# Gate and up products of a feed-forward layer: eight block products replaced by seven with sums

## The reference

```python
def swiglu_ffn(h, wg, wu, wd):
    return (jax.nn.silu(h @ wg) * (h @ wu)) @ wd

# in layer i, for prompt rows (p) and sample rows (s)
fp = swiglu_ffn(xp * (1 + sc2p) + sh2p, ffn_w_gate[i], ffn_w_up[i], ffn_w_down[i])
xp = layer_norm(ALPHA * xp + g2p * fp, ln_ffn_g[i], ln_ffn_b[i])
```

## Time and profile before

| | us |
|---|---|
| three runs | 3110.47, 3113.08, 3115.78 |
| median | 3113.08 |
| span of the profiled execution | 3114.0 |
| busy in the span: PE | 3020.4 |
| DVE | 1431.8 |
| POOL | 1509.5 |
| ACT | 557.7 |

### The profile page before, as it was taken

How to read it: one execution, slowest core, us unless ns; L and a number is a source line. 1 busy time by engine, 2 the same in 40 slices (tenths; PEclk the granted TensorE clock), 3 DMA queues, 4 the chain that set the end, 5 groups by cost and what they waited for, 6 DMA issues and landing times.

```text
span 3114.0 us, 53016 instructions
## 1 busy us (share of the span) xinstructions
PE 3020.4 (97%) x22084; PEld 2794.3 (90%) x22084; DVE 1431.8 (46%) x2529; ACT 557.7 (18%) x1125; POOL 1509.5 (48%) x889
## 2 busy tenths in 40 slices
PE   6999999999999999999989999999999999999997
PEld 4799999999976899999986689999997999999997
DVE  3254652434554752424665545332463536634243
ACT  2220140000220430000234323000022211400001
POOL 2455446545566455545420145554544464455554
PEclk8999999999999999999999999999999999999999
DMA  6642353323345443333321434343322323222221
GB/s 238 223 116 85 119 174 99 107 91 114 90 122 156 152 164 125 132 124 127 87 64 52 116 121 149 128 135 129 116 68 85 100 84 93 80 82 84 82 82 65
DMA packets 450477, 354.81 MB, mean 114 GB/s; under 512 B 26121, under 2 KB 424833, under 8 KB 437934
## 3 DMA queue, kind: packets, MB, share of 16 engines
q1 hardware_dynamic: 435744, 324.79, 32.6%
q10 hardware_dynamic: 14493, 26.63, 2.8%
HBM read 337.86 MB, written 5.25 MB: 110 GB/s over the span
## 4 chain that ended last, share of the span: by engine, by line
issue 33%; PE 30%; POOL 24%; POOLq 10%; DVE 2%; ACT 1%; DVEq 0%; ACTq 0%
PE pb L980 29%; POOL w_lo L890 22%; POOLq L889 10%; POOL prod L916 1%; POOL diag L899 1%; PE pb L1745 0%; PE pb L1702 0%; DVE a_lo L2277 0%; POOLq L945 0%; POOL w_hi L887 0%; POOL yt L946 0%; POOL a_lo L936 0%; DVE xa L2436 0%; DVE pb L2429 0%; PE pb L1624 0%
## 5 line engine op out<-in xcount | busy, mean ns | idle before, releaser
L887 POOL TENSOR_SCALAR w_hi<-w_raw 128x1024 fp32r<-128x1024 f32 (+2 forms) x416 | 449.4, 1080 | 1326.7 <-DMA w_raw<-in_ffn_w_up 399.9
L890 POOL TENSOR_TENSOR w_lo<-w_raw,w_hi 128x1024 fp32r<-128x1024 f32 (+2 forms) x416 | 989.1, 2378 | 69.0 <-issue 69.0
L980 PE MATMUL pb<-h_hi,w_hi 128*128 128x288 f32 x3584 | 946.1, 296 | 10.6 <-DVE xa L2399 3.8
L980 PE MATMUL pb<-h_lo,w_hi 128*128 128x288 f32 x3584 | 927.1, 295 | 0.0
L980 PEld LDWEIGHTS pb<-h_hi,w_hi 128*128 128x128 f32 x3584 | 661.8, 188 | 21.7 <-issue 8.6
L980 PEld LDWEIGHTS pb<-h_lo,w_hi 128*128 128x128 f32 x3584 | 657.6, 188 | 0.0
L980 PE MATMUL pb<-a_hi,w_hi 128*128 128x288 f32 x2176 | 592.9, 297 | 8.1 <-DVE a_lo L2277 5.6
L980 PE MATMUL pb<-a_lo,w_hi 128*128 128x288 f32 x2176 | 587.0, 294 | 0.0
L980 PE MATMUL pb<-h_hi,w_lo 128*128 128x288 f32 x3584 | 560.3, 295 | 0.5
L980 PEld LDWEIGHTS pb<-h_hi,w_lo 128*128 128x128 f32 x3584 | 504.3, 188 | 2.0 <-POOL w_lo L890 1.5
L980 PEld LDWEIGHTS pb<-a_hi,w_hi 128*128 128x128 f32 x2176 | 408.0, 188 | 17.0 <-DVE a_lo L2277 6.7
(11 more groups left out here) (324 smaller groups left out, 2678.9 us busy)
## 6 DMA issues: line engine op xcount, KB each, us to landing
ada_w<-in_ada_w SPq DMA_DIRECT2D x80, 1024.0 KB, 8.0
w_raw<-in_ffn_w_gate SPq DMA_DIRECT2D x88, 512.0 KB, 3.8
w_raw<-in_ffn_w_up SPq DMA_DIRECT2D x88, 512.0 KB, 3.7
w_raw<-in_gmlp_w_in SPq DMA_DIRECT2D x64, 512.0 KB, 4.0
w_raw<-in_ffn_w_down SPq DMA_DIRECT2D x64, 512.0 KB, 3.5
w_raw<-in_gmlp_w_out SPq DMA_DIRECT2D x32, 512.0 KB, 4.5
w_raw<-in_ffn_w_down SPq DMA_DIRECT2D x32, 384.0 KB, 3.1
w_raw<-in_conv_w_pw SPq DMA_DIRECT2D x24, 512.0 KB, 4.0
```

Of the source, the lines that this page charges most:

```text
L887: nc.gpsimd.tensor_scalar(w_hi[:, s, 0:w], w_raw[:, s, 0:w], 1.0, 1.0, ALU.mult, ALU.mult).then_inc(split_hi, 1)
L890: nc.gpsimd.tensor_tensor(w_lo[:, s, 0:w], w_raw[:, s, 0:w], w_hi[:, s, 0:w].bitcast(F32), ALU.subtract).then_inc(split_lo, 1)
L980: return nc.tensor.matmul(out, lhsT, rhs, start=start, stop=stop)
```

## The change

Tiles 0 to 2 of a layer stay as they are, except that tile 2 does its second token half first. From tile 3 on (19 tiles in a layer), the gate and up products of a tile are one product of 2x2 blocks. The weights of a tile are four blocks: the channel halves (four channel tiles each) of gate (g1, g2) and of up (u1, u2). The tokens are four blocks as well: channel half times token half. Eight block products of 4 × 3 matmuls become seven, 84 matmuls in place of 96, by sums of blocks ahead of the products and sums of products behind them:

- weight sums: s1 = u1 + u2, s2 = s1 − g1, s3 = g1 − u1, s4 = g2 − s2
- token sums, once for a layer: t1, t2, t3, t4 in the same pattern; t2 takes the place of the first four channel tiles of the second token half
- products, in the order of PE: p1 = g1·x (first channel and token half), p6 = s2·t2, p5 = s1·t1, p7 = s3·t3, p2 = g2·x (second channel half), p3 = s4·x, p4 = u2·t4
- outputs: c11 = p1 + p2; u23 = p1 + p6; u4 = u23 + p5; c12 = u4 + p3; u23 += p7; c22 = u23 + p5; the fourth is p4 + u23. c11 and c12 are gate, the others up.

DVE makes the weight sums (`form_sums`, `form_last`; s1 and s2 in PSUM banks) and the lower parts of s1 and s2 (`form_low`); ACT makes all upper parts and, in `gated_upper`, those of the gated tile; POOL makes the other five lower parts of 512 words. For the paired tiles POOL no longer makes `w_hi` and `w_lo` of 1024 words. Their units go round slots 0 to 3, the fifth slot holds the sums' parts. Of the token sums DVE makes t1, t3 and t2 and two lower parts, between the splits of tiles 0 and 1 and the gating of tile 2; POOL makes t4 in two operations of 1152 and the lower parts of t3 and t4. DVE also does the sums of products, the gating and the gated tile's lower part (`gated_lower`), in the next tile's turn.

The ada ring becomes four buffers, with other places for its products: four at an FFN's start, then bursts of two to four behind three to five of the tiles, 12 bursts in all. Down products take the last tile of their group late (`late=1`). The residual's scaling on ACT is spread over the first group. The diff, cut to its core; `forms_early` and `forms_late` run on POOL, `form_product` on PE, the loop with `s4_hi` (in `ffn_gates`) on ACT, the rest behind it on DVE, the last lines at each FFN's start:

```diff
-ADA0, ADA1 = 3, 5
+ADA0, ADA1 = 3, 4
...
-ADA_FIRST = 5
+ADA_FIRST = 4
+PAIRED_FROM = 3
+QK = KT // 2
+HALF_UNIT = UNIT // 2
...
+                s = (self.last + 1) % SLOTS
+                if paired and s == SLOTS - 1:
+                    s = 0
...
+            def sums_end(self):
+                self.held[SLOTS - 1] = ("after", (acc_ready, self.products))
...
+            def forms_early(l, m, q):
+                sg_, su = [plan.slot[u] for u in paired_units(l, m)]
+                pool.wait_ge(form_sum, 4 * q + 3)
+                pool.wait_ge(form_hi, 6 * q + 1)
+                lower(w_lo[:, sg_, 0:HALF_UNIT], w_raw[:, sg_, 0:HALF_UNIT], w_hi[:, sg_, 0:HALF_UNIT], form_lo_pool)
+                pool.wait_ge(form_hi, 6 * q + 5)
+                for e in range(2):
+                    part_ = slice(e * HALF_UNIT, (e + 1) * HALF_UNIT)
+                    lower(w_lo[:, su, part_], w_raw[:, su, part_], w_hi[:, su, part_], form_lo_pool)
+            def forms_late(l, m, q):
+                sg_, _ = [plan.slot[u] for u in paired_units(l, m)]
+                pool.wait_ge(form_sum, 4 * q + 4)
+                lower(w_lo[:, sg_, HALF_UNIT:], w_raw[:, sg_, HALF_UNIT:], w_hi[:, sg_, HALF_UNIT:], form_lo_pool)
+                pool.wait_ge(form_hi, 6 * q + 6)
+                lower(s4_lo[:], s4_raw[:], s4_hi[:], form_lo_pool)
...
+                    for m in ms:
+                        forms_late(l, m, FQ.n)
...
+                        FQ.up()
+                        if m != ms[-1]:
+                            forms_early(l, m + 1, FQ.n)
...
+            def form_product(i, wh, wl, xh, xl, lo_made):
+                b = acc_bank()
+                for k in range(QK):
+                    for e, x in enumerate((xh, xl)):
+                        mm(pb[:, b, 0:HALF], wh(k), x(k), k == 0 and e == 0, False)
+                pe.wait_ge(*lo_made)
+                for k in range(QK):
+                    last = mm(pb[:, b, 0:HALF], wl(k), xh(k), False, k == QK - 1)
...
-                        down(count)
+                        down(count, late=1)
                 if l + 1 < DEPTH:
-                    down_norm(GU[2][1])
+                    down_norm(GU[2][1], late=1)
...
+                for m in ms:
+                    act.wait_ge(form_sum, 4 * FQ.n + 4)
+                    fn(s4_hi[:], s4_raw[:], ACT.Copy).then_inc(form_hi, 1)
...
+                    act.wait_ge(acc_ready, G.n + 1)
+                    fn(sg[:, 0, :], pb[:, G.n % BANKS, 0:HALF], ACT.Copy).then_inc(pair_kept, 1)
+                    if m != ms[0]:
+                        gated_upper(m - 1 - first)
...
+                    if m != ms[-1]:
+                        upper_gate(l, m + 1)
+                        upper_up(l, m + 1)
+                        upper_sums(l, m + 1, FQ.n + 1)
+                    for e in range(2):
+                        act.wait_ge(acc_free, BANKS + G.n + 5 + e)
+                        fn(sg[:, e, :], sg[:, e, :], ACT.Silu).then_inc(sg_ready, 1)
...
+                v.tensor_tensor(pb[:, b_1, :], u1, w_raw[:, s_u, HALF_UNIT:], ALU.add).then_inc(form_sum, 1)
+                dve.wait_ge(raw_full[s_g], landed[ug])
+                dve.drain()
+                v.tensor_tensor(pb[:, b_2, :], pb[:, b_1, :], g1, ALU.subtract).then_inc(form_sum, 1)
+                v.tensor_tensor(u1, g1, u1, ALU.subtract).then_inc(form_sum, 1)
...
+            def gated_lower(m):
+                for h in (1, 0):
+                    dve.wait_ge(gated_hi, AH.up())
+                    v.tensor_tensor(one(a_lo, m, half_cols(h)), pr[:, h, :], one(a_hi, m, half_cols(h)).bitcast(F32),
+                                    ALU.subtract).then_inc(a_ready, 1)
...
+            def paired(l, m, ms, first):
...
+                form_last(l, m)
+                if m != ms[0]:
+                    gated_lower(m - 1 - first)
+                dve.wait_ge(pair_kept, q + 1)
+                dve.wait_ge(acc_ready, G.n + 2)
+                dve.drain()
+                v.tensor_tensor(u23, p6, sg[:, 0, :], ALU.add).then_inc(acc_free, 2)
+                dve.drain()
+                dve.wait_ge(acc_ready, G.n + 3)
+                v.tensor_tensor(u4, p5, u23, ALU.add)
+                if m != ms[-1]:
+                    form_sums(l, m + 1, q + 1)
+                dve.drain()
...
+                v.tensor_tensor(u23, p7, u23, ALU.add)
+                dve.drain()
+                v.tensor_tensor(c22, p5, u23, ALU.add).then_inc(acc_free, 2)
...
+                v.tensor_tensor(c11, p2, sg[:, 0, :], ALU.add).then_inc(acc_free, 1)
+                if m != ms[-1]:
+                    form_low(l, q + 1, 1)
...
+                v.tensor_tensor(c12, p3, u4, ALU.add).then_inc(acc_free, 1)
+                if m != ms[-1]:
+                    form_low(l, q + 1, 0)
+                dve.drain()
+                dve.wait_ge(sg_ready, SG.up(2))
+                v.tensor_tensor(c22, c22, sg[:, 1, :], ALU.mult).then_inc(pair_gated, 1)
...
+                v.tensor_tensor(p4, p4, u23, ALU.add)
+                dve.drain()
+                v.tensor_tensor(pr[:, 0, :], p4, c11, ALU.mult).then_inc(acc_free, 1)
...
+                    v.tensor_tensor(t1_raw[:], hf[:, 0], h_hi[:, 0:QK, half_cols(0)].bitcast(F32), ALU.subtract)
+                    dve.drain()
+                    v.tensor_tensor(t1_raw[:], t1_raw[:], h_lo[:, 0:QK, half_cols(0)].bitcast(F32), ALU.subtract)
+                    v.tensor_tensor(t3_raw[:], hf[:, 1], hf[:, 0], ALU.subtract)
+                    dve.drain().then_inc(t_sum, 1)
+                    v.tensor_tensor(hf[:, 1], hf[:, 1], t1_raw[:], ALU.subtract)
+                    dve.drain().then_inc(t_sum, 1)
```

More of the change, by code:

```diff
@@ L503, in __init__, with unit @@
                 self.products, self.v_units = 0, 0
-            def unit(self, *srcs):
+                self.slot, self.prior, self.ordinal = [], [], []
+                self.held, self.last, self.whole = [None] * SLOTS, SLOTS - 1, 0
+                self.sums_free = {}
+            def unit(self, *srcs, paired=False):
+                u = len(self.srcs)
                 self.srcs.append(srcs)
@@ L508, in unit, with sums_begin, free_of @@
                 self.freed.append(None)
-                return len(self.srcs) - 1
+                s = (self.last + 1) % SLOTS
+                if paired and s == SLOTS - 1:
+                    s = 0
+                self.last = s
+                self.slot.append(s)
+                self.prior.append(self.held[s])
+                self.held[s] = u
+                self.ordinal.append(None if paired else self.whole)
+                self.whole += not paired
+                return u
+            def sums_begin(self, l, n):
+                self.sums_free[l, n] = self.held[SLOTS - 1]
+            def sums_end(self):
+                self.held[SLOTS - 1] = ("after", (acc_ready, self.products))
+            def free_of(self, u):
+                before = self.prior[u]
+                if before is None:
+                    return None
+                return before[1] if isinstance(before, tuple) else self.freed[before]
             def product(self, n, *done):
@@ L615, in plan_ffn @@
                         continue
-                    us = [plan.unit(wcols(w, 0, KT, (m + e) * P, P)) for e in range(2 if m == 0 else 1) for w in (wg, wu)]
-                    if m == 0:
+                    if m in (PAIRED_FROM, first) and m:
+                        plan.sums_begin(l, n)
+                    us = [plan.unit(wcols(w, 0, KT, (m + e) * P, P), paired=m >= PAIRED_FROM)
+                          for e in range(2 if m == 0 else 1) for w in (wg, wu)]
+                    if m >= PAIRED_FROM:
+                        plan.product(5, us[0])
+                        plan.product(2, us[1])
+                    elif m == 0:
                         plan.product(4)
@@ L953, in take_units @@
             def take_units(k):
-                slots = [(U.n + n) % SLOTS for n in range(k)]
+                slots = [plan.slot[U.n + n] for n in range(k)]
                 for n, s in enumerate(slots):
-                    unit_in[s] = U.n + n
+                    unit_in[s] = plan.ordinal[U.n + n]
                 U.up(k)
@@ L2608, in down_last, with down @@
                 v.tensor_tensor(yt[0:NS, TT - 1, 0:512], ps, fgb[0:NS, 1, 0:512], ALU.add).then_inc(y_dve, 1)
-            def down(e):
+            def down(e, ahead=None):
                 dve.wait_ge(xa_ready, 16 * (e + 1))
@@ L2614, in down @@
                         add_norm(e, m, h)
+                        if ahead is not None and (m, h) in ((KT - 3, 1), (KT - 1, 0)):
+                            ahead((m, h) == (KT - 1, 0))
             def gated_product(h, q):
@@ new lines, in form_last, with form_low @@
+            def form_last(l, m):
+                s_g = plan.slot[paired_units(l, m)[0]]
+                dve.drain()
+                v.tensor_tensor(s4_raw[:], w_raw[:, s_g, HALF_UNIT:], pb[:, sum_banks[l][1], :], ALU.subtract
```

(12 more changed lines are left out.)

302 lines of the change are left out of this document (256 added, 46 removed).

## The result

The changed kernel took 3127.0 us (median of five, 3122.1 to 3134.2) against 3113.1: **1.0047 times as long, 95% interval 1.0036 to 1.0058**. The forecast was 3104 us, faster as the likeliest sign, in a range of 3060 to 3148. The time lies in the range; the sign was wrong. The profiled execution has a span of 3122.7 us, 8.7 more than before; the forecast's span was 3105.2, 8.8 less than before, and the steps are compared with that.

What follows compares the result with a forecast made beforehand. PE (TensorE) bounds the kernel before; DVE's chain would bound the changed pairs. 3114.0 − 120.8 + 37 + 46 + 22 − 5 + 12 = 3105.2, less 0.9 for the median: 3104 us, range 3060 to 3148.

Steps and rivals of the forecast that it cites:

- Matmuls, −120.8: Paired tiles: 84 matmuls for 96 gain 1.59 us in each of 76 tiles, −120.8 us if PE stays the bound.
- DVE's chain, +37: Paired tiles: DVE's chain of 12.15 us exceeds PE's 11.13, partly hidden by ada bursts; +37 us, bounds 0 and +90.
- A: Rival for the paired tiles: PE stays the bound, with DVE's chain at 10.6 to 11.1 us; 3067 us, chance 0.22.
- B: Rival for the paired tiles: a third DVE wait for POOL, 1.0 us in 52 pairs; 3156 us, chance 0.28.
- Start of an FFN, +46: Each FFN's start: PE waits for added DVE operations and POOL's splits, 11.5 us for a layer, +46 us.
- Weight units, +22: Second down product: its first unit falls into slot 4 and loads late, 5.5 us for a layer, +22 us.
- Late products, −5: Down product starts: taking the last tile late gives PE work while that tile is split, −5 us (4.6 to 5.6).
- Clock, +12: Two idle times in each FFN lower PE's granted clock afterwards, 8 × 1.56 us, +12 us (0 to 16).

Runs made afterwards that it cites:

- The two edits that shorten the chain: Changed kernel with ScalarE's copies for gated tile and product 1 before s4's upper part, 3076.3 us; or two GpSimd lower parts cut to 64 columns, 3077.3 us.
- the free slot: Changed kernel, but tile 2's two units and the first two of each FFN down product never take ring slot 4: 3100.5 us, ratio 0.9954.
- the reordered start: Changed kernel, but VectorE makes token sums t3 and t2 behind the gating of tiles 0 and 1: 3122.5 us, ratio 1.0025.

## Why the prediction was right or wrong

The prediction failed in two steps: the cover of DVE's chain, and the holder of slot 4. By stages, in us against the kernel before, from windows like those above over all four layers:

| | forecast | measured |
|---|---|---|
| matmuls removed | −120.8 | −120.8 |
| DVE's chain in the second and third groups | 32.5 | 52.3 |
| first groups, without the matmuls removed | 57.0 | 62.4 |
| weights of the second down products | 22.0 | 15.0 |
| clock behind that wait | 6.2 | 4.8 |
| last tile late | −5.0 | −5.6 |
| sum | −8.1 | 8.1 |

The first groups' line holds start, pairs and clock: how much longer they are, with 3 × 1.59 added for each, and 0.9 for the wait for a_lo that went in the last layer. The forecast's own sum was −8.8 by rounding. The span grew by 8.7 us, so under 1 us is left; the median of the runs lies 2.5 us above the profiled execution, the fastest and the slowest run 12 us apart.

- **Matmuls, −120.8.** Right: wherever nothing else bounds, the pair takes 11.11 to 11.12 us.
- **DVE's chain, +37: the first step that failed.** The mechanism was right, as was each wait of the pair, and 12.26 to 12.28 for 12.15 is close; rows 7 alone did not show that POOL goes first between two DVE operations, since POOL's operation there begins as its own last one ends, but the 1.93 us after do. Wrong was how far the chain is covered. The forecast let it bind 5 pairs and a share in a group; in the last layer it costs 8.3 and 7.9 us, as much as seven pairs. It let ada bursts hide 17.7 us, and they hide about 12.5. The two edits that shorten the chain give back 51 and 50 us in all. Rivals A and B did not come; either edit turns the last layer into A, and layers 1 and 2 only until weights land too late.
- **Start of an FFN, +46: the second.** The step prices what DVE and POOL add. It doesn't ask who holds slot 4 when the first sums are to be written there, and so puts at nothing a wait for tile 2's last product in layers 1 and 2: 13 us by the windows, 11 by what the free slot gave back there (5.3 and 6.0). The slots had been counted for the down products, but not here. That the whole stage is only 5 us over is partly luck. In layer 0 PE's three waits are 9.2 us where 4.7 + 7.2 were priced: those behind t3's and t4's low parts are 1.0 and not 3.0, that for the bank 3.2 and not 4.2.
- **Weight units, +22.** Right in place, and 5.3 and 5.5 us in layers 0 and 3. "It cannot be hidden" was wrong for layers 1 and 2, where four ada pairs stand behind tile 13 and leave 1.8 and 1.7, and 0.4 more each for w_lo. The 7 us too many hid a part of what the chain lacked.
- **Late products, −5.** −8.6 on the kernel before; as part of the change the term is of another kind, a cover worth 45.6 us, which the forecast named but priced at nothing by itself.
- **Clock, +12.** Too low; its share stands in the stages above. The mean granted clock is 0.983 for 0.991 before. That is 53 us of the span for 28, some 25 more, of which some 20 while PE was at work (worked out from the trace's clock and PE's busy times). In the first groups alone the windows' clocks of 0.97, 0.96, 0.95 and 0.95 stand for some 22 us more than before, idle time included, where one drop of 1.6 us for each was priced: PE waits three or four times in a start, and the clock falls behind more than one of these waits.

With either step's us in it, 20 or 13, the sum would have left the faster side: 3104 + 13 = 3117, and faster began under 3106.9. What stays open is how the ada bursts, the chain and the landing of weights share the time in layers 0 to 2.

## What to carry to other kernels

When a change takes a buffer out of a ring for a new use, go through its first use in every repetition and write down who held it last and when that one is done: the phase of the ring differs from layer to layer, and here the same slot cost nothing in two layers and 5 to 6 us in two others. Where a chain of small operations on one engine is some 10% over the bound, look at the order on the engine that feeds it first: moving three copies ahead of one that nobody needs yet gave 51 us. When a forecast lets one thing hide another, price it in a stretch without the cover first: the last layer, which has no ada products, showed what the chain costs. And a wait that shows at one instruction may have a second cause right behind it, which only moving the first one shows.

## What was not expected of the hardware

The wait between DVE and POOL goes both ways and joins up: in the reordered start POOL's w_lo took 3.28 us for its 2.40 and DVE's t_lo 3.33 for 1.35, each waiting for the other in turn. And a DVE operation with two SBUF inputs and its result in PSUM waits as well, which no row of before had shown and the forecast had taken from the nearest row:

```profile
1159.70 2.67 POOL L1018 TENSOR_TENSOR t_lo<-t_raw,t_hi 128x1152 fp32r<-128x1152 f32 x1
...
1160.21 2.72 DVE L2946 TENSOR_TENSOR pb<-w_raw 128x512 f32<-128x512 f32 x1
```

0.69 us undisturbed, 2.72 here, and it ends 0.56 behind POOL's operation. The Trainium skill, "SBUF — State Buffer", section "Who interferes with whom", makes two SBUF inputs on VectorE, against a GpSimd operation that reads SBUF, the condition of such a wait. It has no word on where the result goes, and the prediction read it as holding for any place; the trace agrees.

The clock fell further behind the wait of 5.33 us than rows 13 show behind 2.69. Two windows of PE behind it (length, busy, clock, DMA, GB/s):

```profile
640.00:644.00 4.00, 4.00 (x18) 0.50 1.21 296
644.00:648.00 4.00, 4.00 (x25) 0.76 0.23 55
```

4 x 0.50 + 4 x 0.24 = 3.0 us. It stood at the lower level (1.2 of 2.4 GHz) for all of the first window and part of the second. But a longer wait is not the whole of it: behind two waits of the same 5.04 us, in layers 0 and 2, the first 4 us of PE differ:

```profile
438.11:442.11 4.00, 4.00 (x20) 0.63 0.25 60
1906.48:1910.48 4.00, 4.00 (x16) 0.50 0.83 199
```

So a drop cannot be priced from one row of before.
